# Eight gate panels of the modulation moved from behind the up blocks to behind up panels of the first half

## The chip, the cores and the metric

The kernel is one program on one NeuronCore of a Trainium2 chip. The metric is the device time of one execution in microseconds, the median over several runs. Five engines run their own instruction streams and meet at semaphores: TensorE (PE in the profile, its weight loads PEld), VectorE (DVE), ScalarE (ACT), GpSimd (POOL) and SyncE (SP), which here only issues the loads of weights.

## The reference, cut to what matters

One decoder layer for a prompt of 256 tokens and 8 sample tokens. Nine modulation vectors come from one product with a weight of 2048 x 18432, and the first of them shape the first norm and the first feed-forward network:

```python
mod = jax.nn.silu(c) @ p['w_ada'][l] + p['b_ada'][l]
sh1, sc1, gt1, shm, scm, gtm, sh2, sc2, gt2 = jnp.split(mod, N_MOD, axis=-1)
h = h + 0.5 * gt1[:, None] * swiglu(modulate(h, p['norm_ffn1'][l], sh1, sc1),
                                    p['w_ffn1_up'][l], p['w_ffn1_down'][l])
# then mixer(modulate(h, ..., shm, scm)), a second feed-forward, a final norm

def modulate(x, gain, shift, scale):
    return rmsnorm(x, gain) * (1.0 + scale[:, None, :]) + shift[:, None, :]

def swiglu(x, w_up, w_down):
    g, u = jnp.split(x @ w_up, 2, axis=-1)
    return (jax.nn.silu(g) * u) @ w_down
```

The shift `sh1` and scale `sc1` must be there before the first norm is complete; the gate `gt1` is first used when the first down product is added to `h`.

## The kernel before, in words

Weights come as panels of 128 x 2048 floats, 1 MB each. SP loads them in a fixed order into a ring of four buffers, `raw`; the load of ring position r waits until position r - 4 has been used (`slot_done`). A weight panel is split into two parts of reduced precision, `whi` on ScalarE (L834, or L980 for a block) and `wlo` on VectorE (L1274, or L1485), each with two buffers. TensorE then does 48 matmuls of 128 x 128 by 264 columns per panel: `whi` with `xhi` and `xlo` (L1968 and L1969, in a block L2136 and L2137), then `wlo` with `xhi` (L1976, L2143). Sums go to four PSUM banks, `acc`. A modulation panel ("ada panel") isn't split: TensorE multiplies it straight from `raw` by the 32 columns of conditions in `csl` (L2043, 8 matmul records a panel, in four column strips of the array) into one bank of `mp`. Four ada panels make a group; a group's sums are copied to `arow` (L857), turned by TensorE (L1953, "fold") and added into `mod`. The gate's panels (groups 8 to 11) are of a kind that is loaded in another layout (L665) and folded only once, after the last of their sixteen.

The first norm needs 32 ada panels (groups 0 to 7). So that TensorE has work before they are all in, the first 16 of the 88 up panels are done as 16 blocks. A block is a quarter of the contraction of four panels. It takes all four banks of `acc`, and its partial sums are then added into `part_g` and `part_u` on VectorE (L1495). Blocks 0 to 3 need the first norm group, blocks 4 to 7 the second, and so on; blocks 12 to 15 finish the sums, and ScalarE and VectorE make the hidden tiles from them. The blocks have two buffers of their own, `blk`, loaded by `load_block`; block b + 2 waits for the `wlo` of block b (`block_lo`). Behind each of blocks 0 to 14 TensorE does two ada panels (`early`), panels 10 to 39: the last eight of these belong to the gate.

After the blocks come the other 28 up panels of the first half, with 16 single ada panels between them, then the down panels of the half, then the second half with 44 up panels and 24 ada panels. These orders are tuples made by `mixed(n, m)`, where a None is an ada panel. Each engine walks the same tuple and each panel's ring position is worked out from it.

The order of instructions of each engine is fixed by this code; no scheduler changes it.

Of the kernel before, what the change touches and what calls it, by code (L numbers as in the profile page):

```python
# [120 lines left out]
UP, FF_DOWN = 4 * UP_IT, 2 * KD  # L121
FF_HALF = UP + FF_DOWN
ADA_FIRST = 2 * KD
# [3 lines left out]
def mixed(n, m):  # L127

    body = [0]
    for x in range(1, n):  # L130
        body.append(x)
        if x < n - 1 and x * m // (n - 2) > (x - 1) * m // (n - 2):
            body.append(None)
    return tuple(body)
# [1 line left out]

BLK = 4
NBLK = BLK * QT
FF1_PLANS = ((mixed(UP - NBLK, 16), 1),), ((mixed(UP, 24), 1),)
FF1_BEGIN = (NBLK, 8, 2), (0, 0, 0)  # L140
QKV_BODY = mixed(CT, 20)
OUT_BODY = mixed(KD, 8)
FF2_PLANS = ((mixed(UP, 12), 1),), ((PLAIN, UP_IT),)
# [1 line left out]
G_FIRST, G_ALL = ADA_FIRST // 4, NADA // 4  # L145
# [23 lines left out]
R_FF1 = ADA_FIRST  # L169
AHEAD = 10  # L170
# [91 lines left out]

def r_start(s):

    return R_FF1 + 8 + s - NBLK


def r_dwa(p):
# [30 lines left out]
def build(nc, t):  # L299
    ctx = ExitStack()  # L300
    with ctx:
# [176 lines left out]
        def sem(name):  # L478
            return ctx.enter_context(nc.semaphore(name))
# [135 lines left out]
        mixed = sem("mixed")  # L615
# [6 lines left out]
        block = ctx.enter_context(nc.Block())  # L622
# [26 lines left out]
        def _(sp):  # L649
# [9 lines left out]
            def load_ada(r, g, p):  # L659
                if not whole(g):  # L660
                    load(r, t["ada"][4 * ada_group(g) + p])
                    return
                first = 4 * (g - g % ATL) + g % ATL
                sp.wait_ge(slot_done[r.slot(RAW)], r.turn(RAW).val())
                sp.dma_start(raw[:, r.slot(RAW), :].rearrange("p (c x) -> p c x", c=ATL),  # L665
                             t["ada"][first:first + 13:4, :, AG * p:AG * p + AG].rearrange("c p x -> p c x"))\
                  .then_inc(panel_loaded[r.slot(RAW)], 16)

            def load_early(k):
                load_ada(At(k), k // 4, k % 4)  # L670

            def load_block(b):
                ph, m = divmod(b, BLK)
                if b >= 2:
                    sp.wait_ge(block_lo, b - 1)
                sp.dma_start(blk[:, b % 2, :].rearrange("p (k c) -> p k c", k=BLK),
                             t["up1"][BLK * m:BLK * m + BLK, :, AG * ph:AG * ph + AG].rearrange("k p c -> p k c"))\
                  .then_inc(block_loaded[b % 2], 16)
# [4 lines left out]
                    load_block(0)  # L683
            load_block(1)
            for b in range(NBLK - 1):
                load_early(AHEAD + 2 * b)
                load_early(AHEAD + 2 * b + 1)
                if b + 2 < NBLK:
                    load_block(b + 2)

# [15 lines left out]
            def bodies(plan, r0, w, w0, g0, early=None, begin=(0, 0, 0)):  # L706
                for body, rounds, p, r, g in stretches(plan, begin):
                    if rounds == 1:
                        body_loads(body, r0 + r, w, w0 + p, g0 + g, 0, early)
                    else:  # L710
                        with sp.Fori(0, rounds) as i:
                            body_loads(body, r0 + r, w, w0 + p, g0 + g, i)

            def ffn(r0, up, down, o, plan, g0, early=None, begin=(0, 0, 0)):
                bodies(plan, r0, up, UP * o, g0, early, begin)
                rd = r0 + plan_end(plan, begin)
                with sp.Fori(0, 4) as i:
                    for k in range(8):
                        load(seq(rd + k, 8, i), down[i * 8 + (FF_DOWN * o + k)], DOWN * P)

            for o in range(2):
                ffn(R_FF1_SECOND if o else R_FF1, t["up1"], t["down1"], o, FF1_PLANS[o], G_FIRST + o * G_FF1_HALF,
                    None, FF1_BEGIN[o])
            bodies(((QKV_BODY, 1),), R_QKV + 4, t["win"], 0, G_QKV, (G_N1,))
# [28 lines left out]
            for part in range(4):  # L753

                sp.wait_ge(out_ready, (part + 1) * KD // 4)
                k = slice(part * KD // 4, (part + 1) * KD // 4)
# [69 lines left out]
        def _(act):  # L826
# [22 lines left out]
            def copy_rows(g, r):  # L849

                if not ends(g):
                    return
                act.wait_ge(slot_done[r.slot(RAW)], (r.turn(RAW) + 1).val())
                if g:

                    act.wait_ge(ada_folded, units(g))
                act.activation(arow[:, :], mp[:, 2, :], ACT.Copy).then_inc(ada_rows, 1)  # L857
# [115 lines left out]
            def start_hi(s):  # L973
                if s >= NBLK:
                    split_hi(At(S_FF1 + s), At(r_start(s)))
                    return
                act.wait_ge(block_loaded[s % 2], 16 * (s // 2 + 1))
                if s >= 2:
                    act.wait_ge(panel_used, s - 1)
                act.activation(whi[:, s % 2, :], blk[:, s % 2, :], ACT.Copy).then_inc(hi_done, 1)  # L980
# [19 lines left out]
            for b in range(NBLK):  # L1000
                start_hi(b + 1)
                block_taken(b)
                if b % 2 == 0:
                    g = 2 + b // 2
                    copy_rows(g, At(4 * g + 3))
                    if g % 2 and g < G_FIRST:
                        norm_group(g // 2)
            start_hi(NBLK + 1)
            for o in range(2):
                ffn(0, o, S_FF1 + o * FF_HALF, R_FF1_SECOND if o else R_FF1, A_FF1 + o * A_FF_HALF,  # L1010
                    FF1_PLANS[o], G_FIRST + o * G_FF1_HALF, False, FF1_BEGIN[o])
            norm(1, SHM, G_N1, R_N1)
# [62 lines left out]
            for g in range(NG):  # L1075
# [16 lines left out]
                for lv in range(LEVELS):  # L1092
                    act.wait_ge(p1_ready, g * LEVELS + lv + 1)
                    act.activation(bD[:, :, :], heads(0), ACT.Copy).then_inc(p1_copied, 1)
                    if lv in HI_AT:
                        k = q + 1 + HI_AT.index(lv)
# [169 lines left out]
        def _(dve):  # L1266
# [244 lines left out]
            for b in range(NBLK):  # L1511
                block_taken(b)
                start_lo(b + 1)
                if b >= NBLK - BLK:
                    block_hidden_tiles(b % BLK, At(A_BLK + BLK * b))
                if b % 2 == 0:
                    g = 2 + b // 2
                    take_ada(g)
                    if g % 2 and g < G_FIRST:
                        dve.wait_ge(ada_taken, g + 1)  # L1520
                        norm_group(g // 2)
            start_lo(NBLK + 1)
            for o in range(2):
                ffn(0, o, S_FF1 + o * FF_HALF, R_FF1_SECOND if o else R_FF1, A_FF1 + o * A_FF_HALF,
                    FF1_PLANS[o], G_FIRST + o * G_FF1_HALF, False, GT1, FF1_BEGIN[o])
            norm(1, SHM, SCM)
# [7 lines left out]
            for x in range(CT):  # L1534
                s, a = At(S_QKV + x), At(A_QKV + x)
# [3 lines left out]
                b = slice(a.slot(BANKS), a.slot(BANKS) + 1)  # L1539
# [90 lines left out]
            for g in range(NG):  # L1630
# [41 lines left out]
                for lv in range(LEVELS):  # L1672
                    if lv in LO_AT:
                        k = q + 2 + LO_AT.index(lv)
# [58 lines left out]
            for c in range(HB // HG + 1):  # L1733
# [9 lines left out]
                if c >= 1:  # L1743

                    b = c - 1
# [117 lines left out]
            for k in range(KD):  # L1863
# [6 lines left out]
                b = slice(a.slot(BANKS), a.slot(BANKS) + 1)  # L1870
# [78 lines left out]
        def _(pe):  # L1949
# [5 lines left out]
            def fresh(a):  # L1955

                pe.wait_ge(acc_taken[a.slot(BANKS)], a.turn(BANKS).val())
# [168 lines left out]
            def block(b, g=None):  # L2126
                ph = b // BLK
                s, a, c = At(S_FF1 + b), At(A_BLK + BLK * b), At(S_FF1 + b).slot(SPLIT)
                pe.wait_ge(hi_done, (s + 1).val())
                pe.wait_ge(x_lo, NB * (ph + 1))  # L2130
                for w in range(BLK):
                    fresh(a + w)
                    for k in range(QT):
                        xh, xl = xs[QT * ph + k]
                        tile = whi[:, c, (QT * w + k) * P:(QT * w + k + 1) * P]
                        mm(to(a + w), tile, xh, start=k == 0, stop=False)  # L2136
                        mm(to(a + w), tile, xl, start=False, stop=False)  # L2137
                    if w == 0 and g is not None:
                        fold(g)
                pe.wait_ge(block_lo, b + 1)  # L2140
                for w in range(BLK):
                    for k in range(QT):
                        last = mm(to(a + w), wlo[:, c, (QT * w + k) * P:(QT * w + k + 1) * P], xs[QT * ph + k][0],  # L2143
                                  start=False, stop=k == QT - 1)
                last.then_inc(panel_used, 1)

            def early(k):
                ada(k % 4, k // 4, At(k))
# [10 lines left out]
            for k in range(8, AHEAD):  # L2159
                early(k)  # L2160
            for b in range(NBLK):
                block(b, 2 + b // 2 if b % 2 else None)
                if b < NBLK - 1:
                    for k in range(AHEAD + 2 * b, AHEAD + 2 * b + 2):
                        early(k)
            for o in range(2):
                ffn(0, o, S_FF1 + o * FF_HALF, R_FF1_SECOND if o else R_FF1, A_FF1 + o * A_FF_HALF,
                    FF1_PLANS[o], G_FIRST + o * G_FF1_HALF, None, FF1_BEGIN[o])
            panels(QKV_BODY, S_QKV, R_QKV + 4, A_QKV, G_QKV, 0,
# [495 lines left out]
```

## Time and profile before

| | us |
|---|---|
| median of 3 runs | 2755.7 (2754.74 to 2759.19) |
| profiled execution | 2755.91 |
| its span | 2754.1 |
| TensorE busy in the span | 2688.7 |
| VectorE busy | 1417.9 |
| ScalarE busy | 1052.7 |
| moved by DMA | 605.58 MB |

The span is what the profiler saw between the first and the last instruction; about 1.8 us of the execution lie outside it. A busy time is the union of an engine's instructions. Matmuls are pipelined, so the start of the next instruction tells better than the end of the last when TensorE went on. Times inside the rows are microseconds from the start of the span.

### The profile page before, as it was taken

To read this page: it belongs to the slowest core of one execution; us is meant where nothing else is said; L and a number is where in the kernel's file an instruction comes from. 1 tells how busy PE (TensorE), PEld (TensorE's weight loads), DVE (VectorE), ACT (ScalarE), POOL (GpSimd) and SP (SyncE) were. 2 spreads that over 40 slices of the span, in tenths; PEclk is the share of its full clock that TensorE was granted. 3 is DMA by queue.
4 is the path that set the end of the run, shared out by engine and by line. 5 is a ranking of instruction groups with operands and counts; after the bars stand their busy time and mean duration, and the time that the engine had idled before them with its cause. 6 is when DMAs were issued, how large, how long until landed. Compare 5 with 4: busy or idle time off the path is not lost.

```text
span 2754.1 us, 49483 instructions
## 1 busy us (share of the span) xinstructions
PE 2688.7 (98%) x21449; PEld 2496.5 (91%) x21449; DVE 1417.9 (51%) x1815; ACT 1052.7 (38%) x1082; POOL 30.3 (1%) x65
## 2 busy tenths in 40 slices
PE   6999999999999899999999999999899999999998
PEld 3789999999999788899988999889799999999998
DVE  3554455444455666455556555375544455444455
ACT  3343333333344323444423444343433333333443
POOL 0000000000000000000010000000000000000000
PEclk8999999999999999999999999999999999999999
DMA  9987755667655887333366665776665655544453
GB/s 377 364 312 259 255 189 188 243 244 262 247 189 186 281 293 282 107 123 123 108 247 225 228 234 203 255 252 242 231 219 209 217 192 181 197 175 181 159 182 133
DMA packets 130832, 605.58 MB, mean 220 GB/s; under 512 B 10720, under 2 KB 10976, under 8 KB 84592
## 3 DMA queue, kind: packets, MB, share of 16 engines
q1 hardware_dynamic: 125584, 582.06, 59.1%
q0 software_dynamic: 4512, 20.59, 2.0%
q8 instruction: 129, 2.11, 0.3%
q10 hardware_dynamic: 576, 0.56, 0.1%
q14 instruction: 31, 0.25, 0.0%
HBM read 590.55 MB, written 12.62 MB: 219 GB/s over the span
## 4 chain that ended last, share of the span: by engine, by line
PE 92%; DVE 3%; ACT 2%; DMA 1%; issue 1%; SPq 0%; DVEq 0%; ACTq 0%
PE acc L1968 24%; PE acc L1969 23%; PE acc L1976 23%; PE mp L2043 4%; PE acc L2225 2%; PE acc L2226 2%; PE acc L2231 2%; PE mp L1953 1%; DMA raw<-in_ada 1%; PE acc L2136 1%; ACT whi L834 1%; PE acc L2137 1%; PE acc L2143 1%; DVE wlo L1274 1%; PE mp L2292 1%
## 5 line engine op out<-in xcount | busy, mean ns | idle before, releaser
L1274 DVE TENSOR_TENSOR wlo<-raw,whi 128x2048 fp32r<-128x2048 f32 (+2 forms) x429 | 893.5, 2083 | 772.7 <-ACT whi L834 772.3
L1968 PE MATMUL acc<-xhi,whi 128*128 128x264 f32 x3840 | 966.2, 289 | 4.5 <-ACT whi L834 4.0
L1969 PE MATMUL acc<-xlo,whi 128*128 128x264 f32 x3840 | 952.0, 286 | 0.0
L834 ACT ACTIVATE whi<-raw 128x2048 fp32r<-128x2048 f32 (+2 forms) x429 | 747.7, 1743 | 531.7 <-PE acc L1976 358.0
L1968 PEld LDWEIGHTS acc<-xhi,whi 128*128 128x128 f32 x3840 | 726.9, 189 | 86.0 <-issue 85.1
L1969 PEld LDWEIGHTS acc<-xlo,whi 128*128 128x128 f32 x3840 | 728.0, 190 | 0.1
L1976 PE MATMUL acc<-xhi,wlo 128*128 128x264 f32 x3840 | 502.5, 284 | 0.0
L1976 PEld LDWEIGHTS acc<-xhi,wlo 128*128 128x128 f32 x3840 | 478.4, 188 | 0.0
L1968 PE MATMUL acc<-uhi,whi 128*128 128x264 f32 x1408 | 348.2, 284 | 0.0
L1969 PE MATMUL acc<-ulo,whi 128*128 128x264 f32 x1408 | 348.0, 284 | 0.0
L1969 PEld LDWEIGHTS acc<-ulo,whi 128*128 128x128 f32 x1408 | 265.3, 188 | 0.0
L1968 PEld LDWEIGHTS acc<-uhi,whi 128*128 128x128 f32 x1408 | 264.7, 188 | 0.0
L1976 PE MATMUL acc<-uhi,wlo 128*128 128x264 f32 x1408 | 192.2, 284 | 0.0
L1976 PEld LDWEIGHTS acc<-uhi,wlo 128*128 128x128 f32 x1408 | 179.8, 188 | 0.0
L2043 PE MATMUL mp<-raw,csl 128*32 128x512 f32 x1152 | 157.5, 630 | 19.0 <-DMA raw<-in_ada 11.2
L922 ACT ACTIVATE uhi<-hf 128x264 fp32r<-128x264 f32 (+1 forms) x80 | 34.1, 426 | 361.9 <-DVE hf L1426 361.9
L915 ACT ACTIVATE sg<-acc 128x264 f32<-128x264 f32 x80 | 31.4, 392 | 273.7 <-PE acc L1976 272.0
L2225 PE MATMUL acc<-xhi,whi 128*128 128x264 f32 x512 | 133.9, 296 | 0.0
L2226 PE MATMUL acc<-xlo,whi 128*128 128x264 f32 x512 | 128.0, 285 | 0.0
L1426 DVE TENSOR_TENSOR hf<-sg,acc 128x264 f32<-128x264 f32 x80 | 34.4, 430 | 137.8 <-PE acc L1976 137.8
L2225 PEld LDWEIGHTS acc<-xhi,whi 128*128 128x128 f32 x512 | 96.6, 189 | 8.4 <-issue 8.4
L2226 PEld LDWEIGHTS acc<-xlo,whi 128*128 128x128 f32 x512 | 96.7, 189 | 0.0
(361 smaller groups left out, 2048.0 us busy)
## 6 DMA issues: line engine op xcount, KB each, us to landing
raw<-in_up SPq DMA_DIRECT2D x160, 1024.0 KB, 4.8
raw<-in_ada SPq DMA_DIRECT2D x144, 1024.0 KB, 7.6
raw<-in_down SPq DMA_DIRECT2D x128, 704.0 KB, 4.1
raw<-in_win SPq DMA_DIRECT2D x69, 1024.0 KB, 6.8
raw<-in_wgate SPq DMA_DIRECT2D x32, 1024.0 KB, 4.8
blk<-in_up SPq DMA_DIRECT2D x16, 1024.0 KB, 6.9
raw<-in_wout SPq DMA_DIRECT2D x16, 1024.0 KB, 6.2
raw<-in_wproj SPq DMA_DIRECT2D x24, 512.0 KB, 5.0
```

The source lines that it names most:

```text
L834: act.activation(whi[:, s.slot(SPLIT), 0:width], raw[:, r.slot(RAW), 0:width], ACT.Copy)\
L915: act.activation(sg[:, u % 2, :], acc[:, a.slot(BANKS), 0:NT], ACT.Silu)\
L922: act.activation(uhi[:, tiles(p // 2 + u, i, per // 2), :], hf[:, u % 2:u % 2 + 1, :], ACT.Copy)\
L1274: v.tensor_tensor(wlo[:, s.slot(SPLIT), 0:width], raw[:, r.slot(RAW), 0:width], whi[:, s.slot(SPLIT), 0:width].bitcast(F32), ALU.subtract)\
L1426: v.tensor_tensor(hf[:, u % 2, :], sg[:, u % 2, :], acc[:, up, 0:NT], ALU.mult)\
L1968: mm(dst, w, xh, start=starts and k == 0, stop=False)
L1969: mm(dst, w, xl, start=False, stop=False)
L1976: last = mm(dst, wlo[:, b, (tile + k) * P:(tile + k + 1) * P], xh, start=False, stop=ends and k == len(xs) - 1)
L2043: last = mm(mp[QR * j:QR * (j + 1), 2, :], csl[:, k, :], raw[:, r.slot(RAW), j * AG:(j + 1) * AG], start=begins, stop=p == KD // QT - 1 an ...
L2225: mm(to(a), w, xh, start=k == 0, stop=False)
L2226: mm(to(a), w, xl, start=False, stop=False)
L2231: last = mm(to(a), wlo[:, b, k * P:(k + 1) * P], xh, start=False, stop=k == KD - 1)
```

## The change

The order is changed at the end of the blocks. Only the 32 ada panels of the first norm remain among the blocks: two behind each of blocks 0 to 10, none behind 11 to 14. The gate's first eight panels go to the 28 up panels of the first half, where 24 single ada panels now stand instead of 16. Ring positions follow. Nothing is computed otherwise, and the number of bytes and of matmuls stays.

```diff
-FF1_PLANS = ((mixed(UP - NBLK, 16), 1),), ((mixed(UP, 24), 1),)
-FF1_BEGIN = (NBLK, 8, 2), (0, 0, 0)
+FF1_PLANS = ((mixed(UP - NBLK, 24), 1),), ((mixed(UP, 24), 1),)
+FF1_BEGIN = (NBLK, 0, 0), (0, 0, 0)
...
-    return R_FF1 + 8 + s - NBLK
+    return R_FF1 + s - NBLK
...
             for b in range(NBLK - 1):
-                load_early(AHEAD + 2 * b)
-                load_early(AHEAD + 2 * b + 1)
+                for k in range(AHEAD + 2 * b, min(AHEAD + 2 * b + 2, ADA_FIRST)):
+                    load_early(k)
                 if b + 2 < NBLK:
                     load_block(b + 2)
...
             for b in range(NBLK):
-                block(b, 2 + b // 2 if b % 2 else None)
-                if b < NBLK - 1:
-                    for k in range(AHEAD + 2 * b, AHEAD + 2 * b + 2):
-                        early(k)
+                g = 2 + b // 2
+                block(b, g if b % 2 and g < G_FIRST else None)
+                for k in range(AHEAD + 2 * b, min(AHEAD + 2 * b + 2, ADA_FIRST)):
+                    early(k)
```

ScalarE's and VectorE's parts of the loop get the same bound (`g < G_FIRST`); for groups 8 and 9 they issued nothing before either.

On TensorE, between block 11 (its last matmuls are L2143) and block 12 (its first are L2136 and L2137), the change is this:

```order
 L2137 MATMUL acc<-xlo,whi 128x264
 L2143 MATMUL acc<-xhi,wlo 128x264 x16
-L2043 MATMUL mp<-raw,csl 32x512 x8
 L2136 MATMUL acc<-xhi,whi 128x264
 L2137 MATMUL acc<-xlo,whi 128x264
```

The pair of ada panels is gone, and the same piece stands three more times, behind blocks 12, 13 and 14.

On SP, before, the end of the blocks' loads and the first loads of the up panels (`blk` is a block, `raw<-in_up` an up panel, `raw<-in_ada` an ada panel):

```order
L676 DMA blk<-in_up 128x4x512
L665 DMA raw<-in_ada 128x4x512 x2
L654 DMA raw<-in_up 128x2048 x3
L665 DMA raw<-in_ada 128x4x512
L654 DMA raw<-in_up 128x2048 x2
```

And the same place after the change, from the last pair of the first norm on:

```order
L654 DMA raw<-in_ada 128x2048 x2
L676 DMA blk<-in_up 128x4x512 x4
L654 DMA raw<-in_up 128x2048 x3
L665 DMA raw<-in_ada 128x4x512
L654 DMA raw<-in_up 128x2048
L665 DMA raw<-in_ada 128x4x512
L654 DMA raw<-in_up 128x2048
```

Four blocks are now loaded one behind the other, and behind the third up panel the loads alternate, one ada panel and one up panel, where before one or two up panels stood between two ada panels. At one place of the 28 two up panels still follow each other.

## Rows read from the trace of the kernel before

**Rows 1.** The page: the span, and the busy time of TensorE with its instructions.
```profile
span 2754.1 us, 49483 instructions
...
PE 2688.7 (98%) x21449; PEld 2496.5 (91%) x21449; DVE 1417.9 (51%) x1815; ACT 1052.7 (38%) x1082; POOL 30.3 (1%) x65
```

**Rows 2.** Windows: each engine's busy time, granted clock, DMA share, GB/s.
```profile
120.00:140.00 20.00, 20.00 (x166) 16.65 (x163) 11.42 (x22) 5.20 (x6) 0.00 (x0) 1.00 1.01 390
...
160.00:180.00 20.00, 18.17 (x145) 14.32 (x138) 12.73 (x23) 7.45 (x12) 0.00 (x0) 1.00 0.95 368
...
220.00:240.00 20.00, 20.00 (x165) 19.02 (x164) 8.35 (x6) 6.62 (x6) 0.00 (x0) 1.00 0.76 284
920.00:980.00 60.00, 58.21 (x470) 50.61 (x466) 38.62 (x65) 18.90 (x16) 1.08 (x2) 1.00 0.88 292
```

**Rows 3.** Chain of waits, 138 to 200 us: start, length, what.
```profile
142.95 1.91 ACT whi L980
...
156.00 14.26 DMA raw<-in_ada
```

**Rows 4.** TensorE in order of time, two pairs of ada panels around block 2.
```profile
61.12 1.92 PE L2043 MATMUL mp<-raw,csl 128*32 128x512 f32 x16
...
68.99 1.92 PE L2043 MATMUL mp<-raw,csl 128*32 128x512 f32 x16
```

**Rows 5.** TensorE in order of time, blocks 12 to 15 and two up panels: first instructions.
```profile
142.83 1.92 PE L2043 MATMUL mp<-raw,csl 128*32 128x512 f32 x16
144.90 0.39 PE L2136 MATMUL acc<-xhi,whi 128*128 128x264 f32 x1
...
150.96 1.06 PE L2043 MATMUL mp<-raw,csl 128*32 128x512 f32 x8
152.78 1.07 PE L2043 MATMUL mp<-raw,csl 128*32 128x512 f32 x8 [0.75 <-DMA raw<-in_ada]
153.78 0.39 PE L2136 MATMUL acc<-xhi,whi 128*128 128x264 f32 x1
...
162.57 0.39 PE L2136 MATMUL acc<-xhi,whi 128*128 128x264 f32 x1
...
171.30 0.39 PE L2136 MATMUL acc<-xhi,whi 128*128 128x264 f32 x1
...
177.94 0.39 PE L1968 MATMUL acc<-xhi,whi 128*128 128x264 f32 x1 [0.53 <-DVE part_g L1495]
...
184.21 0.36 PE L1968 MATMUL acc<-xhi,whi 128*128 128x264 f32 x1 [0.17 <-ACT whi L834]
```

**Rows 6.** Chain of waits, 186 to 215 us: up panels' ends, one ada panel.
```profile
188.36 1.94 PE acc L1976 x16
194.20 1.93 PE acc L1976 x16
...
201.22 1.93 PE acc L1976 x16
```

**Rows 7.** VectorE, then ScalarE, in order of time, behind block 15.
```profile
177.45 0.77 DVE L1495 TENSOR_TENSOR part_g<-acc,part_g 128x264 f32<-128x264 f32 x2 [3.41 <-PE acc L2143]
...
178.82 2.29 DVE L1274 TENSOR_TENSOR wlo<-raw,whi 128x2048 fp32r<-128x2048 f32 x1
...
182.15 1.91 ACT L834 ACTIVATE whi<-raw 128x2048 fp32r<-128x2048 f32 x1
```

**Rows 8.** SP in order of time, the load of block 14; the page, all block loads.
```profile
147.21 0.37 SPq L676 DMA_DIRECT2D blk<-in_up  x1
...
blk<-in_up SPq DMA_DIRECT2D x16, 1024.0 KB, 6.9
```

**Rows 9.** ScalarE in order of time, four successive panels of the QKV stage.
```profile
975.88 1.92 ACT L834 ACTIVATE whi<-raw 128x2048 fp32r<-128x2048 f32 x1 [5.13 <-DMA raw<-in_win]
...
998.69 1.92 ACT L834 ACTIVATE whi<-raw 128x2048 fp32r<-128x2048 f32 x1 [5.84 <-DMA raw<-in_win]
```

More of the change, by code:

```diff
@@ L1002, in _ @@
                 block_taken(b)
-                if b % 2 == 0:
-                    g = 2 + b // 2
+                g = 2 + b // 2
+                if b % 2 == 0 and g < G_FIRST:
                     copy_rows(g, At(4 * g + 3))
-                    if g % 2 and g < G_FIRST:
+                    if g % 2:
                         norm_group(g // 2)
@@ L1515, in _ @@
                     block_hidden_tiles(b % BLK, At(A_BLK + BLK * b))
-                if b % 2 == 0:
-                    g = 2 + b // 2
+                g = 2 + b // 2
+                if b % 2 == 0 and g < G_FIRST:
                     take_ada(g)
-                    if g % 2 and g < G_FIRST:
+                    if g % 2:
                         dve.wait_ge(ada_taken, g + 1)
@@ L2161, in _ @@
             for b in range(NBLK):
-                block(b, 2 + b // 2 if b % 2 else None)
-                if b < NBLK - 1:
-                    for k in range(AHEAD + 2 * b, AHEAD + 2 * b + 2):
-                        early(k)
+                g = 2 + b // 2
+                block(b, g if b % 2 and g < G_FIRST else None)
+                for k in range(AHEAD + 2 * b, min(AHEAD + 2 * b + 2, ADA_FIRST)):
+                    early(k)
             for o in range(2):
```

## The prediction

> **What bounds the kernel now.** I read the page first. TensorE is busy for 2688.7 of 2754.1 us [rows 1], so there are 65.4 us in the whole program in which it has nothing to do, and a change of order can win only from those. Next I read the windows around the place of the change [rows 2]. From 120 to 140 us TensorE is busy throughout and the DMA engines are too, at 390 GB/s. From 160 to 180 us TensorE is busy for 18.17 of 20 us, with the DMA share still at 0.95. From 220 us on, among the up panels, TensorE is busy for 20.00 of 20 us and DMA has room, with a share of 0.76. So the last blocks are a place where DMA ends last, and the up panels behind them a place where TensorE does. The chain of waits names what is late [rows 3]: the `whi` of block 12, which ends at 144.86, and then a stretch of 14.26 us put down to loads of ada panels. Finally the timeline of TensorE gives the starts of the blocks [rows 5], and these carry the sum.
>
> **What is removed: four pairs, behind blocks 11 to 14.** A block lasts from 144.90 to 150.96, that is 6.06 us, counted to the first instruction of what follows [rows 5]. With this length I get what lies between one block and the next.
>
> - Block 11 to 12: the pair starts at 142.83, and block 12 at 144.90, just behind the `whi` that ScalarE ends at 144.86 [rows 3, 5]. That `whi` starts late because ScalarE finishes the fourth norm group first, which the change leaves where it is. Without the pair block 12 starts at 144.86. Gain 0.04: the pair was hidden behind this wait.
> - Block 12 to 13: 153.78 - 150.96 = 2.82. It holds a pair and a wait of 0.75 for the second ada panel's load [rows 5].
> - Block 13 to 14: 162.57 - (153.78 + 6.06) = 2.73.
> - Block 14 to 15: 171.30 - (162.57 + 6.06) = 2.67.
>
> In all 8.26 us go with the pairs.
>
> **What takes their place.** A block uses all four banks, so the next block can start only when VectorE has added the first bank into `part_g`. A pair of ada panels covers that today. Behind block 15, where no pair stands, the price is seen: the block ends at 171.30 + 6.06 = 177.36, and the next panel starts at 177.94, 0.58 us later, released by `part_g` [rows 5]. Three boundaries (12 to 13, 13 to 14, 14 to 15) now pay this: 1.74 us. The boundary 11 to 12 lies behind the `whi`, and 15 to 16 is as before.
>
> Is anything later than `part_g`? Three things could be, and I measure them from a block's end. VectorE's next `wlo` ends at 178.82 + 2.29 = 181.11, 3.75 us behind the end of block 15 [rows 7]. It is needed after 0.58 us and the 32 matmuls with `whi`, two thirds of 6.06, at 4.6 us. ScalarE's `whi` for the block after next starts at 182.15, behind the hidden tiles of the finished block, and ends at 184.06 [rows 7], 6.70 us behind the block's end. It is needed at 0.58 + 6.06 + 0.58 = 7.22 us. That is a slack of 0.5 us. The third is the load of a block. The load of block 14 is issued at 147.21 [rows 8], at the same moment as now, since the `wlo` of block 12 releases it. With the median of 6.9 us it lands at 154.1, and ScalarE asks for it at 150.92 + 4.79 = 155.7. Block 15 is issued when the `wlo` of block 13 is done, at 150.92 + 3.75 = 154.7. It lands at 161.6 and is asked for at 162.35. Both are in time, and the queue is emptier than it is now, since no ada panel stands before them.
>
> The new timeline is then: block 12 at 144.86, block 13 at 144.86 + 6.06 + 0.58 = 151.50, block 14 at 158.14, block 15 at 164.78, the first up panel at 171.42 instead of 177.94. This is 6.52 us earlier, the same as 8.26 - 1.74. The panel after it keeps its distance of 6.27 us (184.21 - 177.94, [rows 5]), because that wait hangs on ScalarE's work behind block 15.
>
> **What is added: eight single ada panels.** They stand between up panels, where TensorE never waits [rows 2]. An up panel alone takes 194.20 - 188.36 = 5.84 us, and one with an ada panel before it 201.22 - 194.20 = 7.02 us [rows 6]. So a single ada panel costs 1.18 us, and eight cost 9.44 us. Nothing hides them. The fold of the gate was in this stretch before and is once there now; it costs nothing new. The down panels wait for the gate only after the last up panel, in both kernels.
>
> A pair costs less than two singles: between the pairs at 61.12 and 68.99 lie one pair and one block, 7.87 us [rows 4], so a pair is worth 7.87 - 5.84 = 2.03 us if a block is taken like a panel. The Trainium skill, "TensorEngine Tiling (Array Packing)", section Key Properties, has a rule for this: a change of the tiling mode drains TensorE, a change of tile in one mode doesn't. The ada matmuls work in column strips of 32 and the others on the whole array, so by this rule eight singles pay for eight switches each way where four pairs paid for four. The trace agrees: 8 x 1.18 = 9.44 against 4 x 2.03 = 8.12. If switches were free, the eight would add 8.12 and the change would cost 1.6 instead of 2.9.
>
> **The loads behind it.** In the dense stretch one ada panel and one up panel, 2.10 MB, are needed every 7.02 us: 299 GB/s. In 120 to 140 us 390 GB/s were moved [rows 2]. The load of an ada panel is issued when the ada panel two before it is used, and the up panel's right behind it. Two transfers at 390 GB/s take 5.4 us. The `whi` of that up panel can end some 10 us after the issue and is needed at 2 x 7.02 = 14.04 us. I take it as hidden, with nearly 4 us of slack.
>
> **The sum.** -6.52 + 9.44 = +2.92 us. Against the profiled execution: the span goes from 2754.1 to 2757.0, the execution from 2755.91 to 2758.8. The median before was 2755.7, 0.2 below the profiled execution, so I predict 2758.6.
>
> **Bounds.** The boundary without a pair costs between 0 (if `part_g` is in time) and the 2.07 us that block 12 waits for `whi` now (144.90 - 142.83, the nearest longer wait). I take 0.58, since it is the same wait at a block's end. Three boundaries: from -1.7 to +4.5 about my sum. The single costs at least half of the pair's 1.92 busy, 0.96: -1.8. Together the ends are -0.6 and +7.4 us, or 2755.1 and 2763.1. Where the loads don't keep up it is more, and that is a rival.
>
> **Rivals.** About 0.2% (5.5 us) is what a measurement of this kernel can tell from no change.
>
> 1. *The dense stretch starves.* The QKV stage has nearly the same order, and there ScalarE waits for loads. The starts of `whi` move from 975.88 to 998.69 in three steps, 7.60 us each [rows 9], while TensorE's step with one ada panel is 7.02. So that stretch eats its slack at 0.58 us a panel. With 4 us of slack it is gone after 7 panels, and the other 17 pay 0.58 each: +9.9, in all +12.8, or 2768.5. Against it: in that stretch the spill of `h` and the conv history move too, and DMA works at a share of 0.88 for 292 GB/s [rows 2]. Here only weights move. Chance 0.08.
> 2. *ScalarE's chain decides at the bare blocks.* The 0.5 us of slack is gone when the hidden tiles and the `whi` are a little later than behind block 15. This decides from 7.22 us on. If each of the three bare boundaries has the wait that block 12 has now, 2.07 instead of 0.58, that is up to +4.5, in all +7.4, or 2763. For it speaks the narrow slack, against it that the same sequence behind block 15 was measured from end to end. Chance 0.08.
> 3. *Faster.* Bare boundaries cost nothing and the block loads' relief shortens the stretch before 142 us, where DMA is at its limit as well [rows 2]. The loads of ada panels 32 and 33, which stood in the queue from some 131 us on, no longer compete with blocks 12 and 13. But block 12 isn't waiting for a load; it waits for ScalarE's norm work [rows 3]. For the kernel to be faster, more than 2.9 us of this would have to be won before block 12. To pass the bound of 0.2% it would take 8.4 us, and the whole stretch from block 11 to block 16 has 8.26 to give. With the waits at 0 and the single at 0.96 I get 2755.1 and no gain. I give 2751, some 4 to 5 us faster, a chance of 0.07, and half of it lies past the bound.
>
> **Chances.** My forecast, a small loss of 2 to 4 us, has 0.77: its own range is 2756.5 to 2761.5. Slower by over 0.2% (over 2761.2) is rival 1, most of rival 2 and a little of the forecast's edge: 0.15. Faster by over 0.2%: 0.04. Within 0.2%: 0.81. The range for 8 in 10 reaches into rival 2 and down to the lower bound: 2754.5 to 2763.
>
> **What the profile after would show.** Block 13 about 6.6 us behind block 12, with an idle of 0.5 us released by `part_g`; the first up panel at about 171.4; no idle of TensorE released by an ada load behind 145 us; DMA share well under 0.9 from 145 to 175 us; 7.02 us for nearly every up panel from 190 to 365 us, none longer except at the fold; and the end of the first half's up panels some 2.9 us later than before. I am wrong if the first up panel starts before 169 or after 174, or if ScalarE's `whi` in the dense stretch makes TensorE wait.

## The result, and where the time went

| | before | changed |
|---|---|---|
| median of 7 runs, us | 2755.7 (2754.55 to 2759.19) | 2765.22 (2760.54 to 2766.41) |
| ratio of the runs | | 1.0027, interval 1.0017 to 1.0037 |
| span of the profiled execution | 2754.1 | 2761.7 |

The changed kernel is slower, by 7.4 us as the ratio has it and by 9.5 us between the medians. The ratio's interval is 4.7 to 10.2 us. The forecast was +2.9 us with a range up to 2763.0, so the sign was right and the size was not, and the time lies outside the range.

The page of the changed kernel, span and first line, answers to [rows 1]:

```profile
span 2761.7 us, 49483 instructions
...
PE 2693.6 (98%) x21449; PEld 2500.4 (91%) x21449; DVE 1417.0 (51%) x1815; ACT 1054.0 (38%) x1082; POOL 30.2 (1%) x65
```

The matmuls are the same 21449, but TensorE is busy 4.9 us longer. Work of the same count that takes longer points to the clock that TensorE is granted. First the place of the change, though. TensorE in order of time, changed kernel, the starts of blocks 12 to 15 and of the first up panel, which answer to [rows 5]:

```profile
143.27 0.39 PE L2136 MATMUL acc<-xhi,whi 128*128 128x264 f32 x1 [2.00 <-ACT whi L980]
...
150.00 0.36 PE L2136 MATMUL acc<-xhi,whi 128*128 128x264 f32 x1 [0.62 <-DVE part_g L1495]
156.71 0.36 PE L2136 MATMUL acc<-xhi,whi 128*128 128x264 f32 x1 [0.62 <-DVE part_g L1495]
163.43 0.36 PE L2136 MATMUL acc<-xhi,whi 128*128 128x264 f32 x1 [0.62 <-DVE part_g L1495]
170.05 0.39 PE L1968 MATMUL acc<-xhi,whi 128*128 128x264 f32 x1 [0.53 <-DVE part_g L1495]
```

The waits are the forecast ones: 2.00 us for the `whi` of block 12 and then 0.62 us for `part_g` at each bare boundary. From block 12 to the first up panel it takes 26.78 us, against 33.04 [rows 5]: 6.3 us saved where 6.5 were forecast. The chain of waits of the changed kernel, one single ada panel between two up panels, answers to [rows 6]:

```profile
193.33 1.93 PE acc L1976 x16
...
200.35 1.93 PE acc L1976 x16
```

The step is 7.02 us, as forecast. Windows of the changed kernel, in the columns of [rows 2]:

```profile
140.00:160.00 20.00, 16.77 (x134) 16.19 (x133) 14.27 (x24) 10.01 (x12) 0.57 (x1) 1.00 0.60 217
160.00:180.00 20.00, 18.71 (x150) 18.13 (x149) 15.28 (x24) 11.45 (x15) 0.00 (x0) 1.00 0.54 209
200.00:240.00 40.00, 40.00 (x321) 34.12 (x321) 16.10 (x12) 12.65 (x12) 0.00 (x0) 1.00 0.92 302
360.00:900.00 540.00, 540.00 (x4400) 516.45 (x4399) 260.62 (x266) 199.39 (x171) 0.00 (x0) 1.00 0.62 219
```

DMA no longer ends last in the last blocks (share 0.60 and 0.54). It is busier in the dense stretch, at 0.92 for 302 GB/s, where TensorE still never waits for a panel's load. The one wait longer than 0.2 us there is 0.25 us at the fold: ScalarE's copy of the gate's sums stands in its queue behind a `whi` that waits for a load. ScalarE, then TensorE, in order of time, changed kernel:

```profile
304.20 1.92 ACT L834 ACTIVATE whi<-raw 128x2048 fp32r<-128x2048 f32 x1 [4.39 <-DMA raw<-in_up]
306.02 0.58 ACT L857 ACTIVATE arow<-mp 128x512 f32<-128x512 f32 x1
...
306.65 0.66 PE L1953 MATMUL mp<-con,arow 128*128 128x128 f32 x4 [0.25 <-ACT arow L857]
```

So up to the down panels the change costs about what was forecast. The chain gives the stretch from the start of block 11's last 16 matmuls to the start of the last 11 of the first down panel. Before:

```profile
140.97 1.94 PE acc L2143 x16
...
364.19 1.35 PE acc L1976 x11
```

And changed:

```profile
139.34 1.94 PE acc L2143 x16
...
366.16 1.35 PE acc L1976 x11
```

That is 223.22 and 226.82 us: +3.6. The first 140 us came out 1.6 us shorter, and that isn't the change's doing: the same point lies between 137.8 and 140.5 us in the later profiles without fillers, in either order. TensorE was at half clock (1.2 GHz) for 17.1 us of them before and for 10.2 us after the change. The other 5.6 us of the 7.6 between the two spans come behind 366 us, where both kernels do the same in the same order. There the granted clock tells it. Windows around the waits for the two later norms and around the gates of the delta rule, before:

```profile
900.00:945.00 45.00, 37.49 (x283) 31.32 (x281) 34.90 (x63) 18.75 (x24) 1.08 (x2) 0.96 0.82 277
1120.00:1170.00 50.00, 48.19 (x304) 43.65 (x303) 24.69 (x48) 21.21 (x25) 0.00 (x0) 0.86 0.29 106
1940.00:1980.00 40.00, 31.61 (x238) 28.59 (x239) 28.33 (x48) 18.41 (x27) 0.00 (x0) 0.91 0.64 221
```

And changed (the last window is put 6 us later, with its stage; the stage in the first window begins 2.0 us later than before, in the same window):

```profile
900.00:945.00 45.00, 37.49 (x263) 31.92 (x262) 33.09 (x60) 19.06 (x26) 1.07 (x2) 0.89 0.76 265
1120.00:1170.00 50.00, 48.18 (x289) 43.23 (x288) 21.89 (x33) 21.49 (x26) 0.00 (x0) 0.83 0.30 107
1946.00:1986.00 40.00, 31.89 (x224) 28.88 (x225) 27.61 (x47) 16.64 (x25) 0.00 (x0) 0.87 0.58 198
```

TensorE's busy time in a window is the same (37.49 in both), but fewer matmuls fit into it: 263 instead of 283. The mean clock is 0.89 instead of 0.96, 0.83 instead of 0.86, 0.87 instead of 0.91. Only 1.2 and 2.4 GHz occur, so this is time at the lower one: behind 900 us, up to the last matmuls, 24 us before and 38 us after. These places are waits or small matmuls in both kernels, and TensorE comes out of them at 1.2 GHz for a while. After the change it is at 1.2 GHz longer. From 360 to 900 us, without a wait, both are at 1.00. The waits themselves aren't longer: all idle time of TensorE behind 366 us adds up to 27.5 us before and 27.3 after.

One of these places shows it in single matmuls. Behind the first two panels of the second feed-forward TensorE waits 2.01 us for a `whi`, in both kernels. The two matmuls behind this wait, before and then changed:

```profile
1965.61 0.36 PE L1968 MATMUL acc<-xhi,whi 128*128 128x264 f32 x1 [2.01 <-ACT whi L834]
1965.80 0.28 PE L1969 MATMUL acc<-xlo,whi 128*128 128x264 f32 x1
```

```profile
1971.79 0.41 PE L1968 MATMUL acc<-xhi,whi 128*128 128x264 f32 x1 [2.01 <-ACT whi L834]
1971.99 0.42 PE L1969 MATMUL acc<-xlo,whi 128*128 128x264 f32 x1
```

The wait is the same, and only in the changed kernel's profile do the matmuls come out of it at 1.2 GHz (0.42 us each instead of 0.28), for 3.4 us.

### The profile page after: what moved, and what is told of

Its sections match the earlier page's. It is cut to its first block, busy times and chain, and to the rows that moved or that the text cites. A ratio compares the mean times of both kernels' runs of the same rounds, so it can differ in the third digit from the quotient of the medians.

```text
span 2761.7 us, 49483 instructions
## 1 busy us (share of the span) xinstructions
PE 2693.6 (98%) x21449; PEld 2500.4 (91%) x21449; DVE 1417.0 (51%) x1815; ACT 1054.0 (38%) x1082; POOL 30.2 (1%) x65
## 4 chain that ended last, share of the span: by engine, by line
PE 93%; DVE 3%; ACT 2%; DMA 1%; issue 1%; SPq 0%; DVEq 0%; ACTq 0%
PE acc L1968 24%; PE acc L1969 23%; PE acc L1976 23%; PE mp L2043 5%; PE acc L2225 2%; PE acc L2226 2%; PE acc L2231 2%; PE acc L2136 1%; PE mp L1953 1%; PE acc L2137 1%; ACT whi L834 1%; PE acc L2143 1%; DVE wlo L1274 1%; PE mp L2292 1%; PE mp L2297 1%
```

## The experiments

Times are medians of 6 to 11 runs. Ratios are to the kernel before, run on the same chip in the same hour, 25 to 34 runs in each comparison; there its median was 2756.6 to 2759.0, so the first 2755.7 was a low sample. Two theories stand against each other. A: the change costs some 4 us of work up to the down panels, and lateness alone moves the stalls of the later stages against the clock. B: the rest is the change's own doing.

**A pure delay of 3.6 us, `shift36`.** The kernel before, with this in the first half behind the tenth up panel:

```diff
+                    if G_FIRST <= g0 <= G_FIRST + 2 and n == UP - NBLK and x == 10:
+                        for _ in range(30):
+                            mm(mp[:, 1, 0:NT], xhi[:, 0, 0:P], xhi[:, 0, :], start=True, stop=True)
```

> The kernel before, with 30 matmuls more (into an unused bank, results unchanged) behind the tenth up panel of the first half: TensorE alone is 30 x 0.12 = 3.6 us later from there on, as it is in the changed kernel; loads, ScalarE and VectorE do what they did. Theory A (clock): of the 9.5 us between the medians only some 3.6 are work in the first half, and the rest comes because the later stages with stalls are met some us later and then run longer at half clock. Then this kernel comes out well over 3.6 us slower than before: 2763 to 2766, with more than the 24 us at half clock behind 900 us that the profile of before has. Theory B (the change's own doing): the rest comes from the new order of loads or panels. Then this kernel is only 3.6 us slower, 2759.3, with the half clock of before.

Measured: 2763.28, ratio 1.0016 (1.0007 to 1.0025), +4.4 us. The time alone would suit theory A, but the kernel before took 2758.92 here and not 2755.7. Taken as a difference, 4.4 us (1.9 to 6.9) agrees with B's 3.6 and falls short of A's 7 to 10. The profile has 31 us at half clock behind 900 us, against 24. That decides nothing either: `before_again` (below) has 31 us too, without a delay.

**Less work at the same places, `light4`.** The changed kernel, which here leaves out most of the work of four gate panels, so that its outputs are not the reference's:

```diff
+                if g in (8, 9) and p in (1, 2):
+                    mm(mp[0:QR, 2, 0:64], csl[:, 0, :], raw[:, r.slot(RAW), 0:64], start=False, stop=False)\
+                      .then_inc(slot_done[r.slot(RAW)], 1)
+                    return
```

> The changed kernel, in which four of the eight moved gate panels are left nearly undone: one matmul of 64 columns instead of four of 512 (so the first gate is not right). Their loads, their places and their switches stay. TensorE saves about 4 x 0.85 = 3.4 us in the first half. Theory A: everything behind comes as early as in the kernel before, and the clock falls as it did there: 2765.2 - 9 = about 2756. Theory B: only the saved 3.4 us: 2761.8.

Measured: 2758.52, ratio 1.0002 (0.9993 to 1.0011). That is +0.6 us to the kernel before (-1.9 to +3.0), near A's 0.3 and away from B's 6.1. Between the first up panel and the down panels it takes 191.49 us against 192.82 in a changed kernel that waits nowhere there (`after_third`), only 1.3 us less: four waits of 1.35 us in all, for a late `whi` and at the fold, took back some of what the thinned panels saved. Yet the kernel is some 6 us faster than the changed one, and in its profile the later stages are as long as in the first profile of the kernel before: 1033.77 us from the QKV stage to the second feed-forward and 794.24 from there to the end. It has the changed order and the changed loads, so these don't lengthen the later stages in every execution.

**TensorE kept busy in the waits, `fill_before` and `fill_after`.** Both kernels got the same edit:

```diff
+            def keep_busy(n):
+                for _ in range(n):
+                    mm(mp[:, 1, 0:2 * P], ident, con[:, C_ID:C_ID + 2 * P], start=True, stop=True)
...
             for k in range(8, AHEAD):
                 early(k)
+            keep_busy(8)
...
                     for m in range(2):
                         ada(m, g, At(r + 2 + m))
+                    keep_busy(8)
...
                     fold(g)
+                    keep_busy(3)
```

> The kernel before, with TensorE kept busy where it stands idle: 8 matmuls more (128x128 by 256 columns of float32, some 0.43 us each, into an unused bank) ahead of block 0 and in the wait for the norm ahead of the QKV stage and ahead of the second feed-forward, and 3 more behind that stage's first two panels. They fit the idle times of 3.7, 4.1, 5.6 and 1.8 us. Theory A: the clock no longer falls in these places (half clock of 43.4 to 50.2, 913.8 to 917.2 and 1944.6 to 1951.4 us goes), worth 3 to 7 us: 2749 to 2753. Theory B says nothing of it; if the clock's fall costs nothing there, the time stays at 2755.7 or rises by up to 3 us where fillers overrun.

> The changed kernel with the same fillers. Theory A: where the clock is held, the shift costs no more than itself, so this kernel is 3 to 5 us above the filled kernel before, not 9.5: 2753 to 2757. Theory B: it stays 9 to 10 us above the filled kernel before.

Measured: 2752.43, ratio 0.9978 (0.9969 to 0.9987), and 2755.86, ratio 0.9993 (0.9984 to 1.0002). The two are 3.4 us apart (3.9 between the means of their 11 executions, 2.4 to 5.4) instead of 6 to 9. Theory A had 3 to 5 here, B 9 to 10. Windows of `fill_before`:

```profile
900.00:945.00 45.00, 42.44 (x309) 34.42 (x308) 35.46 (x65) 17.40 (x24) 1.08 (x2) 1.00 0.85 287
1940.00:1980.00 40.00, 37.75 (x288) 33.39 (x287) 26.34 (x46) 20.78 (x28) 0.00 (x0) 1.00 0.58 205
```

And of `fill_after`:

```profile
900.00:945.00 45.00, 42.44 (x311) 35.41 (x310) 34.11 (x60) 19.32 (x26) 1.07 (x2) 1.00 0.83 282
1940.00:1980.00 40.00, 35.93 (x252) 30.18 (x250) 28.36 (x49) 18.94 (x27) 0.00 (x0) 0.96 0.68 233
```

The clock is 1.00 behind the first of the two waits in both, where it was 0.96 and 0.89. Behind the second it is 1.00 in `fill_before` and 0.96 in `fill_after`, so the fillers don't hold it in every execution. In the waits for the two norms they finish before the wait is over (0.46 to 2.02 us of it are left), so they cost nothing there.

**The changed kernel again, `after_again`, `after_third`, `after_fourth`, and the kernel before, `before_again`.** No edit.

> The changed kernel once more, unaltered, on a chip with 30 or so runs of the kernel before. With a delay alone (30 matmuls, 3.6 us) the ratio was 1.0016, and with fillers the two kernels were 3.4 us apart. Theory A: what the change does is some 3.6 us of work in the first half plus clock, so the ratio is between 1.0013 and 1.0030, and the 9.5 us between the first two medians was partly chance. Theory B: the ratio is 1.0027 or more again, clearly above that of the delay.

> The kernel before, unaltered, as one of the four: ratio 1.000 within 0.001, which shows what the comparison resolves. Its profile is a second sample of the stages. Theory A (the change adds 4.2 us up to the down panels and the rest of the difference is how the half-clock stretches fall in an execution): from the first matmul of the QKV stage to that of the second feed-forward it takes between 1032 and 1038 us, from there to the end 794 to 797, as the kernels of both kinds have had. Theory B (the change makes the later stages slower): 1032 to 1036.5 and 794 to 795.

> The changed kernel, a third sample. Both theories: ratio 1.0015 to 1.0030. Theory A: the later stages' times vary from execution to execution, and at least one of this sample and the next has less than 1036.5 us from QKV to the second feed-forward. Theory B: again 1037.5 and 796.4, as in its first two profiles.

> The changed kernel, a fourth sample, with the same expectations as the third.

Measured: `after_again` 1.0024 (1.0015 to 1.0033), `after_third` 1.0033 (1.0020 to 1.0045), `after_fourth` 1.0030 (1.0019 to 1.0041), `before_again` 1.0001 (0.9993 to 1.0010). So the change costs 6.6 to 9 us, and the first result was no accident. It is more than `after_third` was expected to show (up to 1.0030). `before_again` falls into the ranges of both theories, and so do the later stages of `after_third` in part: its 1035.28 us is as A had it, its 796.47 as B had it. Each profile gives the stages anew (us, each the difference of two starts on TensorE, the last one to the end of its last matmul; "clock" says whether TensorE was at half clock in block 12):

| | block 11's last part to down panels | QKV to second feed-forward | from there to the end | clock |
|---|---|---|---|---|
| before | 220.55 | 1033.77 | 794.50 | no |
| before_again | 220.99 | 1036.21 | 794.32 | no |
| changed | 224.14 | 1037.52 | 796.46 | no |
| after_again | 225.24 | 1037.63 | 796.42 | yes |
| after_third | 223.68 | 1035.28 | 796.47 | no |
| after_fourth | 226.15 | 1036.81 | 796.58 | yes |
| shift36 | 224.93 | 1036.45 | 794.22 | no |
| light4 | 223.87 | 1033.77 | 794.24 | yes |

The 552.32 us between the down panels and the QKV stage are the same in all of them, within 0.01. The means of the changed kernel less those of before are +4.0, +1.8 and +2.1, in all 7.9 us. Two profiles of before are few for this: `before_again` has 31 us at half clock behind 900 us where the first has 24, and the changed kernel has 38, 38, 31 and 38.

The granted clock of the other executions is on record as well, as a mean over each. A mean lower by 0.001 means 2.8 us of TensorE at full speed less. In the three comparisons above that have it for both kernels, the changed kernel's 24 executions have a mean of 0.9892 and the 59 of the kernel before 0.9904. The mean time is 6.9 us longer (5.6 to 8.2), and 3.4 us of that (2.3 to 4.6) is missing clock, at most, since clock that is missing in a wait costs nothing. The rest, at least 3.5 us, is what the changed order costs as work.

In two of the four profiles of the changed kernel the clock falls right behind the 2.00 us for which TensorE stands in front of block 12, bare now of its pair. Window of `after_again` there:

```profile
139.00:149.00 10.00, 8.01 (x54) 7.79 (x53) 6.38 (x12) 6.53 (x7) 0.57 (x1) 0.83 0.62 216
```

Block 12 then takes 8.27 us to the start of block 13 instead of 6.73: 1.5 us more. With `light4`, `fill_after` and `after_delay17` it is five of the seven profiles that have this wait unfilled; in the profiles with the pair in it the clock never falls there.

**That wait filled too, `fill_after12`.** `fill_after` with `keep_busy(4)` ahead of block 12.

> The changed kernel with the fillers of fill_after and 4 more matmuls (1.7 us) in the wait of 2.0 us ahead of block 12, where the profile of fill_after had a stretch at half clock (142.9 to 146.3 us) and that of the changed kernel had none. Theory A: in the executions in which the clock falls there, 1.7 us come back: 0 to 1.7 us below fill_after's 2755.9, ratio to before 0.9987 to 0.9993. Rival: the filler delays block 12 and it is 0 to 1 us slower.

Measured: 2756.0, ratio 0.9992 (0.9984 to 1.0001). The wait ahead of block 12 is down to 0.26 us, and block 13 starts 6.75 us behind block 12, without the fall. The median shows no gain over `fill_after`; 1.5 us in some of the executions is less than the comparison resolves.

**Half of the change, `keep36`, and a thinner spread, `spread36`.** Both keep 36 ada panels among the blocks and put 20 behind up panels:

```diff
-FF1_PLANS = ((mixed(UP - NBLK, 24), 1),), ((mixed(UP, 24), 1),)
-FF1_BEGIN = (NBLK, 0, 0), (0, 0, 0)
+FF1_PLANS = ((mixed(UP - NBLK, 20), 1),), ((mixed(UP, 24), 1),)
+FF1_BEGIN = (NBLK, 4, 1), (0, 0, 0)
...
+BEHIND = (2, 2, 2, 2, 2, 2, 2, 2, 2, 2, 2, 2, 1, 1, 0, 0)   # spread36; keep36: thirteen 2, then 0
```

> Half of the change: the pairs behind blocks 11 and 12 stay, only those behind 13 and 14 go, and the first half gets four single ada panels more (20) instead of eight. From the trace of the changed kernel: the two bare boundaries save 2.73 - 0.67 and 2.67 - 0.67, and four singles cost 4.8 us: +0.7 us in the first half. If the hidden pair behind block 11 is what made the change dear, this is 2.9 us below the whole change; rival: cost goes with the number of moved panels, then half of 3.6, +1.8.

> Pairs behind blocks 0 to 11, one ada panel behind 12 and 13, none behind 14, and 20 singles in the first half. One ada panel covers the wait for part_g and leaves the loads time, so the boundaries behind 12 and 13 shrink from 2.8 to about 1.2 us: -1.6 - 1.5 - 2.0 + 4.8 = -0.3 us, the same as before. Rival: the single's load is still late there (0.7 us each): +1.1 us.

Measured: `keep36` 2758.79, ratio 1.0004 (0.9996 to 1.0013); `spread36` 2753.69, ratio 0.9985 (0.9976 to 0.9994). To the down panels they take 223.36 and 221.24 us, against 220.55 and 220.99 before. For `keep36` that is +2.6 where +0.7 was expected, a miss: the pairs that stay wait longer for their loads, 1.51 us behind block 11 and 1.44 behind block 12, where the first profile of before has no wait and 0.75. Its time is only 1.1 us (-1.1 to +3.6) above before, because its QKV stage to the second feed-forward is the shortest of all unfilled profiles, 1032.26 us, with only 24 us at half clock behind 900; that part is luck of one execution. TensorE in order of time, `spread36`, from block 12 on:

```profile
143.95 1.07 PE L2053 MATMUL mp<-raw,csl 128*32 128x512 f32 x8 [1.58 <-DMA raw<-in_ada]
...
150.98 1.07 PE L2053 MATMUL mp<-raw,csl 128*32 128x512 f32 x8
...
158.02 1.07 PE L2053 MATMUL mp<-raw,csl 128*32 128x512 f32 x8
...
165.75 0.36 PE L2146 MATMUL acc<-xhi,whi 128*128 128x264 f32 x1 [0.62 <-DVE part_g L1505]
```

The pair behind block 11 waits 1.58 us for a load here too, but one ada panel behind block 12 or 13 covers the wait for `part_g` and finds its load in time. Blocks 12 to 14 start 7.03 and 7.04 us apart, as dense as up panels with a single. The kernel is 4 us faster than before, though its first half is no shorter; that gain isn't explained by the stages I measured, and its one profile is of one of its longer executions (2757.36). By the mean clocks of its 11 executions 2.0 of 3.9 us (1.0 to 3.0) are clock; the other half stays open.

**Both together, `fill_spread36`.**

> The two edits that made the kernel faster together: the order of spread36 (pairs behind blocks 0 to 11, one ada panel behind 12 and 13, none behind 14, 20 singles in the first half) and the fillers of fill_before. Singly they gave ratios of 0.9985 and 0.9978. If they add, 0.9965 (2749); if the order's gain was mostly chance, since its first half is as long as before (221.2 against 220.6 to 221.3 us), 0.9978 as with the fillers alone.

Measured: 2751.4, ratio 0.9983 (0.9974 to 0.9991). It is faster than both kernels, but no better than the fillers alone can be told to be (0.9978): the gains don't add.

**Lateness alone, once more: `delay42` and its twin `delay42_b`, `delay17`, `after_delay17`.** The edit of `shift36` with 34, 34 and 14 matmuls on the kernel before, and with 14 on the changed one.

> The kernel before with 34 matmuls more behind the tenth up panel of the first half: 34 x 0.12 = 4.1 us of lateness and nothing else, which is what the changed kernel has at its down panels (224.8 against 221.0 us from block 11's last matmuls, on average, +3.8 to +4). Theory A: lateness alone makes the later stages slower, through where the stalls meet the clock: ratio 1.0024 to 1.0033 as for the change, and from the second feed-forward to the end 796.4 us. Theory B: the rest comes from the change itself: ratio 1.0015, 794.3 us.

> The same kernel as delay42, a second sample of its time and of its stages; the same expectations.

> The kernel before with 14 matmuls more at the same place, 1.7 us of lateness. Theory A: the loss is no straight line in the lateness: the total is anything from 0 to 5 us above before, with other stretches at half clock than before in the profile. Theory B: ratio 1.0006 and the later stages as in before.

> The changed kernel with 14 matmuls more at the same place, 1.7 us later. Theory A: the later stages no longer take 796.5 us from the second feed-forward to the end in every execution; the total is not 1.7 us above the changed kernel but between 1 us below and 5 above, ratio to before 1.0020 to 1.0040. Theory B: 1.7 us above: ratio 1.0034, with 796.5 us.

Measured: 1.0014 (1.0005 to 1.0023), 1.0015 (1.0006 to 1.0024), 1.0007 (0.9998 to 1.0017), 1.0026 (1.0016 to 1.0037). Around the second norm's wait the clock falls once in some executions and twice in others, the second time behind the wait of 2.01 us for a `whi` that all have. `delay17`, then `delay42_b`:

```profile
1940.00:1980.00 40.00, 30.97 (x212) 26.29 (x212) 26.14 (x49) 18.93 (x27) 0.00 (x0) 0.87 0.67 225
```

```profile
1943.00:1983.00 40.00, 31.27 (x237) 27.12 (x236) 28.22 (x48) 18.68 (x28) 0.00 (x0) 0.91 0.65 224
```

With 0.87 the rest of the program takes 796.42 us, with 0.91 794.24. So the longer form of this stretch (796 us) is met with the old order too (`delay17` and `delay42`, 796.27; `keep36` has 796.55), which answers half of theory A. The other half fails: on average a delay of 4.1 us costs 4.0 us, not 7, and by the mean clocks of these 22 executions 0.9 us (-0.6 to +2.4) of missing clock come with it, not 3.4. `delay17` has B's ratio (1.0006) with A's long stage. And 1.7 us on top of the changed kernel cost nothing that can be seen: 2766.39 against 2765.2; its ratio is in A's range and under B's 1.0034, though its last stage is 796.45 us, as B had it.

These profiles also give the old order more samples. Less their delays (3.59, 4.07, 4.07 and 1.68 us, by the stretch from the first up panel to the down panels) they take 221.3 to 222.0 us in the table's first column, because the loads of the pairs behind blocks 11 to 14 are later in them. The mean of all six is 221.4, and the changed kernel's +4.0 becomes +3.4. The second and third columns come down to +1.0 and +1.5.

## Why the forecast was wrong, point by point

- *Three bare boundaries at 0.58, pairs worth 8.26.* Right. The waits are 0.62 us, the starts 6.71 to 6.73 apart where 6.64 was forecast, and the saving is 6.3 instead of 6.5 us. Nothing else was later than `part_g`; rival 2 did not happen. The saving was read from one execution that was good to the old order: from block 12 to the first up panel the kernel before took 33.04 us there and 33.49 in `before_again`, and up to 34.45 in the delayed kernels, whose delay stands behind this stretch: the pairs' loads came later.
- *Eight singles at 1.18.* Right: from the first up panel to the down panels 192.82 us (`after_third`, where the fold doesn't wait), against 183.42 or 183.41, is +9.40 for a forecast of 9.44. Eight halves of a pair would be 8.12. The Trainium skill, "TensorEngine Tiling (Array Packing)", section Key Properties, says that a change of tiling mode drains TensorE; the measured 9.40 agrees with that. Not foreseen was the fold that waits behind a late `whi`: 0.25 us in the first profile, where the stretch is 193.28, and 0.7 in those of `fill_after` and `after_fourth`, where it is 193.74. It adds 0.5 and 0.9 us to the step.
- *Boundary 11 to 12, "gain 0.04".* The start was right and the consequence was missed. The pair was not only hidden, it kept TensorE busy. With it gone TensorE stands for 2.00 us, and in two of four profiles the clock falls: 1.5 us, some 0.7 on average. The bounds took 2.07 us for block 12's wait before the change, but from 142.83 to 144.90 TensorE was at work on the pair [rows 5]; that the bare wait came to 2.00 is no merit of that reading.
- *The loads, rival 1.* TensorE never waited for a panel in the dense stretch. DMA's share was 0.92, nearer the edge than the 4 us of slack suggest, and the late `whi` at the fold is the sign of it.
- *The step that failed is the sum itself*, which took everything outside the place of the change as fixed. It had no term for the clock. The local sum of +2.9 is what the profile without the fold's wait and without the fall at block 12 has (`after_third`, 223.68 us against 220.55 and 220.99). The kernel lost 6.9 us on average, and up to 3.4 of them are clock: some 0.7 at block 12, and by the profiles the rest in stages that the change doesn't touch, as more time at 1.2 GHz behind the waits for the two later norms and around the delta rule's gates. The profile of before showed that these waits cost clock (0.96, 0.86, 0.91 in the windows above); I read the page's row of nines and didn't look at them. With 3.4 us for it the sum would have been +6.3.

Shown is that the later stages differ by the clock (the same matmuls, idle time of 27.5 and 27.3 us, a lower mean clock, and the stretch without waits equal to 0.01 us), that the kernels draw together when the waits are filled (3.4 us), and that the changed order isn't needed for the longer form (`delay17`) and doesn't force it (`light4`). Open is why the changed kernel meets the longer form (796 us from the second feed-forward to the end) in each of its four profiles, while of the four profiles with the old order and a delay two have it, and these kernels cost just their delay. It has two stalls that those lack, 2.00 us at block 12 and the bare boundaries, but I didn't separate these from the lateness.

## What to carry to other kernels

When work is moved, ask first what it was standing in. A pair of small matmuls in an unavoidable wait costs nothing and keeps TensorE's clock up; the same pair among full panels costs its whole time, and the bare wait that it leaves can bring the clock down on the work behind it (1.5 us behind a wait of 2.00 here). Where a kernel has waits that end at half clock, any change of a few microseconds ahead of them carries an error of a few microseconds behind them: look at the granted clock there before you name a range, and measure a pure delay of the same size as a yardstick. Filling such waits with idle matmuls was worth 0.2% here.

## What the runs showed that I had not expected

- Matmuls that compute nothing made the kernel faster: 30 of them, some 13 us of TensorE's time, gave 2752.43 for 2758.92 in the same comparison.
- Behind a wait of 2.00 us in front of block 12 the clock was down to 1.2 GHz in some executions of one program and not in others, with the time from block 13 to the first up panel equal to 0.02 us.
- The wait of 2.01 us in the second feed-forward is in all 14 profiles without fillers. In eight of them the clock falls behind it, and the program takes 796.3 to 796.6 us from that stage's start to the end. In the other six it doesn't, and that takes 794.2 to 794.5 us.
